# Slot 1's expert weights loaded from a list through Pool's queue, and its order of blocks reversed

## The reference, cut to what matters

```python
def expert_block(args):
    xblk, e = args
    hid = jax.nn.silu(xblk @ w_gate[e]) * (xblk @ w_up[e])
    return hid @ w_down[e]
```

## Time and profile before

| what | value |
|---|---|
| median of three runs | 4387.5 us (4382.78 to 4392.72) |
| the profiled execution's own time | 4384.98 us |
| its span | 4383.2 us |
| PE busy | 3946.5 us, 90% |
| DVE, ACT, POOL busy | 1444.3, 898.6, 125.6 us |
| mean granted TensorE clock | 0.961 |
| DMA traffic | 693.44 MB, mean 158 GB/s |
| blocks stages, roughly | 2526 to 3144 and 3719 to 4310 us |

### The profile page before, as it was taken

How to read it: one execution, slowest core, us unless ns; L and a number is a source line. 1 busy time by engine, 2 the same in 40 slices (tenths; PEclk the granted TensorE clock), 3 DMA queues, 4 the chain that set the end, 5 groups by cost and what they waited for, 6 DMA issues and landing times.

```text
span 4383.2 us, 48965 instructions
## 1 busy us (share of the span) xinstructions
PE 3946.5 (90%) x19350; PEld 1970.3 (45%) x19351; DVE 1444.3 (33%) x2688; ACT 898.6 (21%) x1885; POOL 125.6 (3%) x203
## 2 busy tenths in 40 slices
PE   4997888899999889999988799999799997999986
PEld 2555665454444555444664333333344443333333
DVE  2485666313302663252463411111231114111115
ACT  3003454202001332121152211111120002111111
POOL 0000000000000000000000000000100000000001
PEclk8998999999999999999999899999899998999997
DMA  6310222110101000110240299999711103999995
GB/s 244 136 39 36 94 94 112 44 42 33 62 20 39 1 1 10 48 46 30 97 156 20 84 399 378 426 426 424 312 36 39 39 21 130 385 391 392 420 423 200
DMA packets 81279, 693.44 MB, mean 158 GB/s; under 512 B 9696, under 2 KB 11560, under 8 KB 45408
## 3 DMA queue, kind: packets, MB, share of 16 engines
q10 hardware_dynamic: 39824, 342.78, 19.0%
q1 hardware_dynamic: 23168, 280.66, 16.0%
q0 software_dynamic: 18128, 67.77, 4.2%
HBM read 636.11 MB, written 55.05 MB: 158 GB/s over the span
## 4 chain that ended last, share of the span: by engine, by line
PE 44%; DMA 11%; DVE 4%; issue 1%; ACT 1%; POOL 0%; ACTq 0%; DVEq 0%; POOLq 0%
PE banks L259 22%; PE banks L2345 12%; DMA arena<-in_w_gu 10%; PE banks L2362 5%; PE banks L1476 1%; DMA arena<-y_tok,arena 1%; DVE arena L1591 1%; PE banks L2329 1%; PE banks L2067 1%; PE banks L2352 1%; DMA arena<-h_tok,arena 1%; PE banks L466 1%; PE banks L1545 0%; PE banks L1525 0%; DVE banks L1590 0%
## 5 line engine op out<-in xcount | busy, mean ns | idle before, releaser
L259 PE MATMUL banks<-arena 128*128 128x512 f32 (+2 forms) x4544 | 1752.2, 547 | 50.4 <-ACTq L138 28.7
L259 PEld LDWEIGHTS banks<-arena 128*128 128x128 f32 x4544 | 841.6, 191 | 950.4 <-issue 887.5
L2345 PE MATMUL banks<-arena 128*64 128x512 f32 x3136 | 718.4, 615 | 70.8 <-DMA arena<-in_w_gu 68.5
L2345 PEld LDWEIGHTS banks<-arena 128*64 128x64 f32 x3136 | 231.4, 142 | 548.2 <-issue 456.8
L2362 PE MATMUL banks<-arena 128*64 128x512 f32 x1568 | 349.2, 598 | 3.2 <-issue 3.2
L1545 PE MATMUL banks<-arena 128*64 128x128 f32 x1952 | 162.1, 285 | 54.5 <-ACT arena L1558 39.3
L2362 PEld LDWEIGHTS banks<-arena 128*64 128x64 f32 x1568 | 109.0, 137 | 208.5 <-issue 208.5
L939 DVE SCALAR_TENSOR_TENSOR arena<-arena 128x1024 f32<-128x1024 f32 x240 | 195.9, 878 | 0.2 <-DVEq L138 0.2
L2435 DVE COPY arena<-banks 128x256 f32<-128x256 f32 x98 | 41.1, 420 | 414.4 <-PE banks L2352 414.4
L1476 PE MATMUL banks<-arena 64*128 64x256 f32 (+2 forms) x768 | 130.1, 469 | 37.8 <-ACT arena L1647 32.8
L301 DVE SCALAR_TENSOR_TENSOR arena<-banks,arena 128x512 f32<-128x512 f32 (+1 forms) x72 | 51.9, 721 | 333.7 <-PE banks L259 333.7
(11 more groups left out here) (341 smaller groups left out, 3075.3 us busy)
## 6 DMA issues: line engine op xcount, KB each, us to landing
arena<-in_w_gu ACTq DMA_DIRECT2D x98, 2048.0 KB, 14.0
arena<-in_w_dn ACTq DMA_DIRECT2D x49, 2048.0 KB, 13.2
arena<-in_w_gu SPq DMA_DIRECT2D x42, 2048.0 KB, 12.3
arena<-in_w_ada SPq DMA_DIRECT2D x24, 2048.0 KB, 7.3
arena<-in_w_dn SPq DMA_DIRECT2D x21, 2048.0 KB, 14.9
y_tok<-arena ACTq DMA_DIRECT2D x196, 128.0 KB, 12.7
y_tok<-arena POOLq DMA_DIRECT2D x1, 16384.0 KB, 45.2
arena<-in_ab_w_ada SPq DMA_DIRECT2D x6, 2048.0 KB, 9.4
```

The lines of the kernel that those rows point to most:

```text
L259: last = pe.matmul(self.bank_of(g, n), lhsT, rhs, start=k == 0, stop=k == KT - 1)
L2345: last = pe.matmul(bank(2 + s_)[64 * h:64 * h + 64, :], xbT[:, k, 64 * s_:64 * s_ + 64], w_gu[s_][:, k, h], start=k == 0, stop=k == KT - 1 ...
```

## The change

1. **Order.** Slot 1 takes its blocks from the end: round j has block 2n-1-j, so it begins with the experts that have fewest blocks. `blk_of`, `places` and the results' addresses (`dest16`, by five more linked DVE operations) follow.
2. **A list for slot 1.** `fresh2` marks new experts for either slot, `one_l` becomes two lists; `moe_tab` gets the experts and first rounds of both (`AT_E`, `AT_POS`), and for slot 1 the round in which each expert ends (`AT_END`). PE's wait for slot 1's weights goes by rank in the list, as slot 0's does.
3. **Queue.** ACT issues no loads any more. Pool does: after the gather of round 1 it loads the first expert, and for each further one it first makes the gathers up to one round beyond the change, then issues parts a and b, then down, each when its part is free.
4. `row_ix` gets one more column, and one more gather is made than before, whose rows nobody uses; Pool waits for it at the end.

```diff
@@ PE's tables
-                pe.matmul(bank(7)[0:NBLK, 128:129], c("before")[0:NBLK, 0:NBLK], fresh, start=True,
+                pe.matmul(bank(7)[0:NBLK, 128:130], c("before")[0:NBLK, 0:NBLK], fresh2, start=True,
...
-                for at_, col in ((AT_E, exp_id), (AT_POS, place[:, 2:3])):
-                    pe.matmul(bank(7)[0:1, at_:at_ + LOADS], col, one_l, start=True, stop=True)
-                pe.matmul(bank(7)[0:1, AT_EXP:AT_EXP + NBLK], exp_id, ident[0:NBLK, 0:NBLK], start=True, stop=True)
+                both_l = one_l.rearrange("p a b -> p (a b)")
+                for at_, col in ((AT_E, exp_id), (AT_POS, place[:, 0:1])):
+                    pe.matmul(bank(7)[0:1, at_:at_ + 2 * LOADS], col, both_l, start=True, stop=True)
+                pe.matmul(bank(7)[0:1, AT_END:AT_END + LOADS], place[:, 0:1], one_l[:, 1], start=True, stop=False)
+                pe.matmul(bank(7)[0:1, AT_END:AT_END + LOADS], place[:, 1:2], held, start=False, stop=True)
@@ DVE's chain
-                link(d.tensor_scalar(blk_of, side, rounds_n[0:NBLK], first_round, ALU.mult, ALU.add))
-                link(d.tensor_scalar(cmp_b[0:NBLK], upto, blk_of, None, ALU.is_lt))
+                link(d.tensor_scalar(n_last, rounds_n, 2.0, -1.0, ALU.mult, ALU.add))
+                link(d.tensor_scalar(blk_of, side, n_last[0:NBLK], from_end, ALU.mult, ALU.add))
+                link(d.scalar_tensor_tensor(out=before_of, in0=side, scalar=2.0, in1=blk_of, op0=ALU.mult, op1=ALU.add))
+                link(d.tensor_scalar(cmp_b[0:NBLK], upto, before_of, None, ALU.is_lt))
...
+                for s_ in range(2):
+                    link(d.tensor_scalar(one_l[:, s_], c("iota", NBLK)[:, 0:LOADS], rank2[:, s_:s_ + 1],
+                                         fresh2[:, s_:s_ + 1], ALU.is_equal, ALU.mult))
+                link(d.tensor_tensor(rank2, rank2, fresh2, ALU.add))
+                link(d.tensor_scalar(held, c("iota", NBLK)[:, 1:LOADS + 1], rank2[:, 1:2], valid, ALU.is_equal,
+                                     ALU.mult))
+                link(d.tensor_tensor(rank, rank2[:, 1:2], rank2[:, 0:1], ALU.subtract))
+                d.tensor_scalar(rank, rank, side, rank2[:, 0:1], ALU.mult, ALU.add).then_inc(m_oh, 1)
...
+                link(d.tensor_scalar(n_last, rounds_n, 3.0, -1.0, ALU.mult, ALU.add))
+                link(d.tensor_scalar(bef16, blk16, rounds_n, None, ALU.is_ge))
+                link(d.tensor_scalar(rank16, blk16, -2.0, n_last, ALU.mult, ALU.add))
+                link(d.tensor_tensor(rank16, rank16, bef16, ALU.mult))
+                link(d.tensor_tensor(blk16, blk16, rank16, ALU.add))
@@ blocks_pool
-                with g.Fori(0, n) as j:
-                    g.wait_ge(self.xt, j + 1)
-                    self.gather(g, j + 1)
+                more = g.value_load(moe_tab[0:1, AT_ROUNDS + 1:AT_ROUNDS + 2], min_val=1, max_val=LOADS - 1)
+                e = g.value_load(moe_tab[0:1, AT_E + LOADS:AT_E + LOADS + 1], min_val=0, max_val=E - 1)
+                g.wait_ge(self.xt, 1)
+                self.gather(g, 1)
+                for part in range(2):
+                    self.load_gu(g, 1, e, part)
+                self.load_dn(g, 1, e)
+                with g.Fori(0, more) as i:
+                    first = g.value_load(moe_tab[0:1, bass.ds(AT_POS + LOADS + i, 1)], min_val=0, max_val=ROUNDS - 1)
+                    end = g.value_load(moe_tab[0:1, bass.ds(AT_END + i, 1)], min_val=1, max_val=ROUNDS)
+                    e = g.value_load(moe_tab[0:1, bass.ds(AT_E + LOADS + 1 + i, 1)], min_val=0, max_val=E - 1)
+                    with g.Fori(first, end) as j:
+                        g.wait_ge(self.xt, j + 2)
+                        self.gather(g, j + 2)
+                    for part, free in ((0, self.free_a), (1, self.free_b)):
+                        g.wait_ge(free, 2 * end + 2)
+                        g.sem_inc(self.passed, 1)
+                        self.load_gu(g, 1, e, part)
+                    g.wait_ge(self.free_d, 2 * end + 2)
+                    g.sem_inc(self.passed, 1)
+                    self.load_dn(g, 1, e)
+                first = g.value_load(moe_tab[0:1, bass.ds(AT_POS + LOADS + more, 1)], min_val=0, max_val=ROUNDS - 1)
+                with g.Fori(first, n) as j:
+                    g.wait_ge(self.xt, j + 2)
+                    self.gather(g, j + 2)
+                g.wait_ge(self.xg, 16 * n + 32)
+                g.sem_inc(self.passed, 1)
@@ blocks_pe
-                    need = [16 * rank_ + 16, 16 * j + 16]
+                    need = [16 * ranks[0] + 16, 16 * ranks[1]]
@@ round_act becomes the body of a plain loop in blocks_act
-                if not last:
-                    a.wait_ge(self.free_a, 2 * j + 4)
-                    self.load_gu(a, 1, e, 0)
...
-                if not last:
-                    self.load_gu(a, 1, e, 1)
...
-                if not last:
-                    a.wait_ge(self.free_d, 2 * j + 4)
-                    self.load_dn(a, 1, e)
```

More of the change, by code:

```diff
@@ L1986, in program @@
         blk_of, exp_of, exp_bf, fresh, valid, rank = (mem(M0 + 7463 + i, 1, n=NBLK) for i in range(6))
-        one_l = mem(M0 + 7470, LOADS, n=NBLK)
-        places = mem(M0 + 7510, 2, ROUNDS + 1)
+        one_l = mem(M0 + 7640, 2, LOADS, n=NBLK)
+        held = mem(M0 + 7704, LOADS, n=NBLK)
+        fresh2, rank2 = (mem(M0 + 7736 + 2 * i, 2, n=NBLK) for i in range(2))
+        before_of, n_last = mem(M0 + 7740, 1, n=NBLK), mem(M0 + 7741, 1)
+        places = mem(M0 + 7510, 2, ROUNDS + 2)
         dest16 = mem(M0 + 7580, 16)
@@ L2099, in route_pe @@
                     for s_ in range(2):
-                        last = pe.matmul(bank(0)[64 * s_:64 * s_ + 64, 0:ROUNDS + 1], at_off[:, n], in_blk[:, n, s_],
+                        last = pe.matmul(bank(0)[64 * s_:64 * s_ + 64, 0:ROUNDS + 2], at_off[:, n], in_blk[:, n, s_],
                                          start=n == 0, stop=n == 15, skip_group_check=True)
@@ L2217, in route_dve @@
                 link(d.tensor_copy(ends, bank(7)[:, 0:65]))
-                first_round, side = (c("place", NBLK)[:, i:i + 1] for i in range(2))
+                first_round, side, from_end = (c("place", NBLK)[:, i:i + 1] for i in range(3))
                 upto = ends[0:NBLK, 32:64]
@@ L2335, in blocks_pe @@
                 with pe.Fori(0, n) as j:
[L2336 to L2337 removed]
+                    ranks = [pe.value_load(moe_tab[0:1, bass.ds(AT_RANK + 2 * j + s_, 1)], min_val=1, max_val=LOADS)
+                             for s_ in range(2)]
+                    need = [16 * ranks[0] + 16, 16 * ranks[1]]
                     pe.wait_ge(self.xe["A"], j + 1)
@@ L2409, in blocks_act @@
                 n = self.rounds(a)
-                before = a.value_load(moe_tab[0:1, AT_ROUNDS + 1:AT_ROUNDS + 2], min_val=1, max_val=ROUNDS - 1)
-                e = self.expert(a, 0)
-                a.wait_ge(self.xg, 16)
-                for part in range(2):
-                    self.load_gu(a, 1, e, part)
-                self.load_dn(a, 1, e)
-                self.copy_x(a, "A", 0)
-                with a.Fori(0, before) as j:
-                    self.round_act(a, j, False, n)
-                self.round_act(a, before, True, n)
+                self.copy_x(a, "A", 0)
+                with a.Fori(0, n) as j:
+                    for s_ in range(2):
+                        a.wait_ge(self.free_b, 2 * j + s_ + 3)
+                        a.activation(sg[:, s_], bank(2 + s_)[:, 0:256], ACT.Silu).then_inc(self.sg, 1)
+                    self.copy_x(a, "A", j + 1)
+                    a.wait_ge(self.free_d, 2 * j + 3)
+                    a.wait_ge(self.yw[0], 32 * j + 32)
+                    a.activation(y_sb[:, 0], bank(6), ACT.Copy).then_inc(self.ye[0], 1)
+                    a.wait_ge(self.ye[0], j + 2)
+                    self.store_y(a, 0, j)
+                    a.wait_ge(self.ye[1], j + 2)
+                    self.store_y(a, 1, j + n)
                 for s_ in range(2):
```

64 lines of the change are left out of this document (23 added, 41 removed).

## The result

The changed kernel takes **4458.9 us** (median of 4 runs, 4456.7 to 4464.8) where the kernel before, on the same chip, takes 4385.1 (4 runs, 4374.7 to 4392.7): ratio 1.0172, interval 1.0148 to 1.0196. It is slower by 74 us. The forecast was slower by 158.

What follows compares the result with a forecast made beforehand. It took PE and DMA as both nearly full, with 101.4 us lost in block rounds. Rounds net +145, first rounds +10.4 and routing +2.6 gave +158 on 4384.98: 4543 us, range 4435 to 4655.

Steps and rivals of the forecast that it cites:

- pairs near 50 us at the end of layer 0: Sign of being right: two successive rounds take about 59 us before round 17 of layer 0, near 50 after.
- part a starts at 16.3 + 7.7 = 24.0 at the earliest: Slot 1's part a queues behind the gather, issued at 16.3 us into the round and taking at least 7.7 to land.
- Preparing and plain rounds: Slot 1 new, slot 0 not; preparing if SP loads slot 0 for the next round: 129 us; plain otherwise: 12 us.
- Dual rounds: Rounds where both slots need new weights: part a 3.4 us late, 5.2 with the lower clock; 18 rounds, 94 us.
- gather, down part and a store end together at 27.5: In dual rounds these share the DMA engines from 20.7, 2.88 MB in 6.8 us; part a then lands at 32.7.
- The last dual round of layer 0: It also shares bandwidth with two next-stage units that SP issues: 14.4 us plus 1.8 for the clock, 16 us.
- First rounds: Each layer's first round: part a stands behind gather 1, 5.2 us late; 10.4 us for both layers.
- Pool's end of the stage: Pool's final wait for one more gather: lands before the last stores, 0 us; 2 if uncovered.
- 2.6 for routing: Some 11 more small DVE links per layer, six ahead of the tables: 1.3 us a layer, 2.6 in all.
- A: Rival, faster: gather and loads start promptly, part a before about 21, preparing and plain rounds lose nothing; 4327 us, chance 0.08.
- B: Rival, slower by less: queues hardly hurt each other in preparing rounds, 15 x 1.7 us instead of 129; 4440 us, chance 0.17.
- C: Rival, slower by more: Pool's stream slower (+57 us), part b also at the lower clock (+59); 4659 us, chance 0.10.

Runs made afterwards that it cites:

- rev_pool_late: Changed kernel's order and routing, slot 1's loads in every round on Pool's queue, parts a and b behind the gather, against the kernel before: 4475.6 us.
- rev_pool_early: Changed kernel's order and routing, slot 1's loads in every round on Pool's queue, parts a and b ahead of the gather, against the kernel before: 4367.7 us.
- old_late: Kernel before, with ACT's loads of slot 1's parts a and b moved behind its copy of the next tokens, some 16.5 us into the round: 4429.8 us.
- rev_act: Changed kernel's order and routing, but ACT issues slot 1's loads in every round as in the kernel before: 4385.0 us.
- list_pool_early: Also "the early list": changed kernel with its 43-load list, parts a and b issued on Pool's queue ahead of the last gather, once free: 4352.1 us.
- list_pool_22: Changed kernel, with slot 1's parts a and b held until slot 1's down products have ended (22.4 us into the round): 4638.6 us.
- list_pool_19: Changed kernel, with slot 1's parts a and b held until slot 0's down products have ended (19 us into the round): 4534.9 us.

## Why the prediction was right and wrong, by its own steps

**Right: the direction and its cause.** The loads behind the gather cost more than six loads fewer bring. The forecast's mechanism, a late issue that leaves too little time, is what rev_pool_late against rev_pool_early shows, and old_late against the kernel before. Right too: 43 loads; slot 1's part a issued about 17.5 into the round (17.3); pairs near 50 us at the end of layer 0 (copies 3112.88 to 3166.89 are 54.0 with the last dual round, the two pairs before it 51.4 and 48.9); a DMA mean well below 407 GB/s (342; I wrote about 320); the granted clock below 0.97 (0.95 and 0.96 in the two stages). Order and routing cost nothing that rev_act can show (its interval reaches from nothing to 8 us); a freed ACT it doesn't test, since there ACT still issues the loads. The six loads that vanish are real but late in the order: the early list gains 15.6 us over the same kernel without it.

**Wrong: the size, 74 for 158.** The step that failed is "part a starts at 16.3 + 7.7 = 24.0 at the earliest", with the gather's lag read as a property of Pool's queue ("none of 51 landed in less than 7.7"). They had been issued in stages where the DMA engines were at 0.97 of their time. In the changed kernel 36 of 53 land in 4.2 to 5.7 us, nearly all of them issued into idle engines, just because the loads come late; the 17 at 10.6 to 11.9 are the first of either layer and those issued while SP's parts are under way. In the quiet round shown, slot 1's packets begin at 19.9, not 24.0. Two of the forecast's own signs of being wrong are there: intervals of 22.4 in plain and preparing rounds, and a part a that lands 9.7 us behind the gather's issue in that round; the pairs before round 17 take 54 to 55 us, not 59. The change itself took away the load under which the lag had been measured. The same thing shows the other way in rev_pool_early, where the engines are full: its gathers need 9.1 at least, 13.9 in the median.

From that step the terms went in both directions:

- *Preparing and plain rounds*: 129 + 12 = 141 forecast, **7.1** measured. Part a is there at 26.0 (29.8 in the forecast), and b at 32.5, not 39.6: in time.
- *Dual rounds*: 94 + 16 = 110 forecast, **161.9** measured, 8.5 each. The step that failed here is that gather, down part and a store end together at 27.5. I had part a land at 32.7; in the round shown PE waits for it until 35.6 (2924.62). The gather shares the engines with SP's part b first (queue q1 moves 1.51 MB from 2905.4 to 2910) and lands at 28.2; SP's down part lands only at 33.4 (issued 2908.45, 14.0 us) and goes on beside part a. The wait for slot 1's down product and the lower clock over both parts came on top (I gave 1.8; it is 2.7). The last dual round of layer 0 costs 9.2, not 16.
- *First rounds*: 10.4 forecast, 4.9 measured.
- *Pool's end of the stage*: 0 forecast, 2 if uncovered; 4.7 measured in both layers together. The Pool-issued lists, which all make the extra gather, have 13.3 to 14.1 us from last down products to first gather; rev_pool_early and rev_pool_late, which load through Pool without it, and all ACT-issued versions have 11.4.

141 - 7.1 is 134 too much, 161.9 - 110 is 52 too little, 5.5 too much in the first rounds, and the 2.6 for routing don't show: 90 in all. 158 - 90 = 68 is what the rounds show (67.5), beside the 4.7 at the stages' ends. Errors of both signs stand in this sum; that the time still lies inside the stated range is luck.

Worked round by round, I also missed a plainer account of the duals. A pair needs 49.2 us of transfer. When slot 1's loads are issued late, the engines run dry once a pair, and the pair shown lasts 54.8, 5.6 more. By this account it doesn't matter in which of its two rounds the delay appears; no run tests that by itself. It fits list_pool_22: between copies 2973.02 and 3037.64 of it lie 64.6 us, 15.4 over 49.2, in which the share of the DMA engines is 0.82 and the rate 329 GB/s, so that some 12 us are idleness.

**The rivals.** A set its decision point near the truth (a before about 21: it is 19.9) and its claim for preparing and plain rounds holds, yet it forecast 4327: it gave the duals 2.0 each, and they cost 8.5. B's time, 4440, is nearest of all, and it had the preparing rounds nearly free, but not by its mechanism: queues do hurt each other where they meet, as list_pool_22's preparing round shows. C's slower Pool stream is excluded by the early versions; nor was Pool held up in issuing, which took 0.54 to 0.60 us in all 86 cases. Had the start been at 24.0, the sum would have been too small, not too large: part a's packets begin at about 21.3 in the quiet round looked at in list_pool_19 (2972, counted from 2950.6) and 24.7 in list_pool_22, and these cost 155 and 259, so 24.0 lies near 240 by interpolation. The bound of 54 us per microsecond of lateness was of the right size: 58 from 19.9 to 21.3, 31 from there to 24.7.

The Trainium skill's rule ("DMA: Bandwidth & Descriptors", Anatomy of one DMA, SWDGE path), an estimated 3.2 us for a gather, is what I set aside because the trace's minimum was 7.7. Where nothing else moves, the measured 4.2 to 5 are nearer to the rule than to that minimum; beside other queues' traffic (11.5 in old_late, 16.2 at most in the kernel before) it is far off. I had compared the rule with loaded engines only.

## What to carry to other kernels

A latency read from a trace belongs to the load under which it was taken; when a change alters that load, look for the same operation in the trace's idle stretches, or bound it by both. The load that counts is what moves beside it, not what moves when it is issued. Where transfers set the pace, the question of a moved issue isn't "how late does this tile land" but "do the engines run dry, and for how long per period". In a queue that carries a gather and weight loads, issue the loads as soon as their buffer is free and let the gather, which has slack, stand behind them: that order, with the earlier hour that it brings, was worth 102 us here with the list, and 108 with a load in every round.

## What the runs showed of the hardware

Pool's software queue carried weights at least as well as ACT's hardware queue. With every load early, rev_pool_early is 17 us faster than rev_act on the same chip (ratios 0.9970 and 1.0009 to the kernel before, intervals apart); with the list, 0.9932 stands against 0.9959, and the intervals overlap. I had not expected a gain, and its cause isn't settled. It lies in the dual rounds, whose excess over 22.40 is 83.6 us in rev_pool_early and 103.3 in rev_act. What differs besides the queue is that Pool waits for nothing of ACT's between its loads; no run separates the two.

The pair of list_pool_early from 2880.84 to 2928.42 takes 47.6 us, less than the 49.2 that 426 GB/s allow for 21.0 MB. The rate in it is 426 GB/s, so only 20.3 MB moved between its two copies; the rest must have moved before or after.

Also open: no run issues the late list in one queue with the gather in another, which would test G directly. The nearest are old_late (gather alone in Pool's queue, loads issued at 16.5, 52 us) and rev_pool_late (gather ahead of the loads in one queue, 95 us), but they differ in more than that.
